# First norm's weight as one row spread by a matmul, convolution blocks split in column halves with rounded products first, small bank copies ahead of the statistics

## The reference

```
h    = rms_norm(x, mix_norm)                      # the first norm
proj = h @ w_in     # u | v | z | xBC | dt | gate_a | gate_b
y_a  = sgu_branch(u, v)        # gelu; layer_norm(v); u * (W_s v + b) in groups of 128
y_b  = mamba2_branch(z, xBC, dt)   # causal conv + silu on xBC, chunked scan, gated norm
x    = x + (sigmoid(gate_a) * (y_a @ w_branch_a) + sigmoid(gate_b) * (y_b @ w_branch_b)) @ w_out
x    = x + moe_ffn(rms_norm(x, ffn_norm))         # 32 experts, top 4, clamped SwiGLU
x    = x + sigmoid(rms_norm(x, ple_norm) @ w_ple_gate) * (p @ w_ple_proj)
out  = rms_norm(x, final_norm)
```

## Time and profile before

| | |
|---|---|
| median of 3 runs | 1320.26 us |
| profiled execution, its own time | 1319.52 us |
| its span, first to last instruction | 1317.5 us |
| PE busy / PEld busy | 1236.3 us (94%) / 654.5 us (50%) |
| DVE / ACT / POOL busy | 351.2 (27%) / 236.2 (18%) / 188.2 us (14%) |
| read from HBM | 456.29 MB, 347 GB/s over the span |
| chain that ended last | DMA 48%, PE 47%, DVE 2%, the rest 3% |

### The profile page before, as it was taken

The page is one execution under the profiler, slowest core; times in us unless marked ns, Lnnn a source line. Parts: engine busy times, 40 slices in busy tenths (PEclk is TensorE's granted clock), DMA queues, the critical chain, the costliest instruction groups (busy, mean ns, idle before and its releaser), DMA issues.

```text
span 1317.5 us, 15399 instructions
## 1 busy us (share of the span) xinstructions
PE 1236.3 (94%) x6309; PEld 654.5 (50%) x6309; DVE 351.2 (27%) x672; ACT 236.2 (18%) x283; POOL 188.2 (14%) x55
## 2 busy tenths in 40 slices
PE   5998999987999999999999999999999999999976
PEld 5986888865444444443334433333334433333342
DVE  3528650434112112121111221211112211211132
ACT  4654444422001000010000000100000000100011
POOL 5855548830000000000000000000000000000000
PEclk9988999997799999999999999999999999999989
DMA  8543357755599999999999999999999999999910
GB/s 266 191 135 122 127 184 298 282 188 226 219 415 428 429 429 428 428 428 428 429 430 429 427 428 428 429 429 429 428 428 428 429 429 429 428 428 428 428 70 32
DMA packets 61350, 457.67 MB, mean 347 GB/s; under 512 B 6800, under 2 KB 16368, under 8 KB 36752
## 3 DMA queue, kind: packets, MB, share of 16 engines
q1 hardware_dynamic: 61328, 457.36, 84.5%
HBM read 456.29 MB, written 1.05 MB: 347 GB/s over the span
## 4 chain that ended last, share of the span: by engine, by line
DMA 48%; PE 47%; DVE 2%; issue 1%; ACT 1%; SPq 0%; POOL 0%; DVEq 0%; ACTq 0%
DMA wring<-in_w_dram 46%; PE bank L825 15%; PE bank L586 6%; PE bank L587 6%; PE bank L588 6%; PE bank L855 4%; PE bank L802 3%; PE bank L926 2%; PE bank L811 1%; PE bank L573 1%; PE bank L690 1%; PE bank L874 1%; PE bank L712 1%; DMA z<-in_mix_norm_dram 0%; PE bank L831 0%
## 5 line engine op out<-in xcount | busy, mean ns | idle before, releaser
L825 PE MATMUL bank<-wring,hT 128*64 128x512 f32 x2048 | 456.8, 599 | 29.0 <-DMA wring<-in_w_dram 29.0
L825 PEld LDWEIGHTS bank<-wring,hT 128*64 128x64 f32 x2048 | 140.4, 137 | 324.0 <-issue 256.5
L855 PE MATMUL bank<-wring,xbcT 128*64 128x512 f32 x1024 | 226.8, 595 | 0.0
L547 POOL TENSOR_TENSOR blk_lo<-blk,blk_hi 128x2048 fp32r<-128x2048 f32 (+1 forms) x41 | 185.9, 4545 | 88.5 <-ACT blk_hi L944 75.8
L855 PEld LDWEIGHTS bank<-wring,xbcT 128*64 128x64 f32 x1024 | 70.7, 137 | 152.1 <-issue 152.1
L1485 DVE TENSOR_SCALAR xbcT<-bank 128x512 f32<-128x512 f32 x32 | 22.1, 692 | 463.2 <-PE bank L831 463.2
L802 PEld LDWEIGHTS bank<-xbcT,ga 128*128 128x128 f32 x1056 | 126.2, 196 | 5.1 <-issue 2.3
L802 PE MATMUL bank<-xbcT,ga 128*128 128x64 f32 x1056 | 124.9, 278 | 1.8 <-issue 1.8
L1104 ACT ACTIVATE xbcT<-xbcT 128x512 f32<-128x512 f32 x32 | 20.2, 630 | 501.4 <-DVE xbcT L1485 501.4
L944 ACT ACTIVATE blk_hi<-blk 128x2048 fp32r<-128x2048 f32 x39 | 74.6, 1915 | 112.8 <-DMA blk<-in_w_in_dram 71.7
L1499 DVE COPY xbcT<-bank 128x256 f32<-128x256 f32 x32 | 13.6, 425 | 270.7 <-PE bank L860 270.7
(11 more groups left out here) (229 smaller groups left out, 944.5 us busy)
## 6 DMA issues: line engine op xcount, KB each, us to landing
wring<-in_w_dram SPq DMA_DIRECT2D x192, 2048.0 KB, 21.7
blk<-in_w_in_dram SPq DMA_DIRECT2D x28, 1024.0 KB, 5.2
blk<-in_w_branch_a_dram SPq DMA_DIRECT2D x4, 1024.0 KB, 5.1
blk<-in_w_branch_b_dram SPq DMA_DIRECT2D x4, 1024.0 KB, 6.1
blk<-in_w_out_dram SPq DMA_DIRECT2D x4, 1024.0 KB, 5.1
blk<-in_w_ple_gate_dram SPq DMA_DIRECT2D x4, 1024.0 KB, 9.1
x<-in_x_dram SPq DMA_DIRECT2D x4, 512.0 KB, 5.1
v<-in_w_ple_proj_dram SPq DMA_DIRECT2D x1, 1024.0 KB, 9.0
```

The lines of the kernel that those rows point to most:

```text
L547: nc.gpsimd.tensor_tensor(dst, raw, hi.bitcast(FP32), ALU.subtract).then_inc(done, 1)
L825: last = mm(bank[dh * SLOTS:(dh + 1) * SLOTS, :], xgT[:, k, :], wring[:, 2 * c + kk, off + dh * W:off + (dh + 1) * W], start=(k == 0), sto ...
L855: last = mm(YB[dh * SLOTS:(dh + 1) * SLOTS, :], actT[:, kk * P + c * SLOTS:kk * P + (c + 1) * SLOTS], wring[:, at, (kk % 2) * D + dh * W:( ...
```

## The change

Three things are changed, and nothing else in the kernel.

1. The weight of the first norm is loaded as one row into one partition, as the first DMA, instead of as 128 copies behind x. PE spreads it over the partitions by two matmuls with a row of ones into banks 6 and 7; DVE applies the norm from there, in halves of 512 columns, and PE starts to transpose a half as soon as it is there. Both sums of squares are made by ACT.
2. The eight xBC blocks are rounded and subtracted in two column halves each. PE makes the eight products of rounded with rounded for a column half first, then those with `blk_lo`, then those with a_lo, and the first column half of block 0 is rounded ahead of a_hi.
3. DVE's small bank copies are placed between the statistics of v's first half and those of its second.

```diff
-            for t in range(TT):
-                load(x[:, t, :], x_in[0, t * P:(t + 1) * P, :], x_loaded[t])
-            load(mix_gain, vec(mix_norm), mix_loaded)
+            load(mix_row, mix_norm, mix_loaded)
+            for t in range(TT):
+                load(x[:, t, :], x_in[0, t * P:(t + 1) * P, :], x_loaded[t])
...
+            pe.wait_ge(mix_loaded, 16)
+            for h in range(HALVES):
+                last = mm(banks[6 + h][:, :], ones[0:1, :], mix_row[:, h * W:(h + 1) * W], start=True, stop=True)
+            last.then_inc(gain_spread, 1)
             for t in range(TT):
-                pe.wait_ge(xn_done, t + 1)
                 for h in range(2):
+                    pe.wait_ge(xn_done, 2 * t + h + 1)
                     transposes(("xT", t, h), ...)
-            wait_taken(pe, *all_of("xT"))
+            pe.wait_ge(act_high, 4)
...
-                        pe.wait_ge(xbc_low, i + 2 if i else c + 1)
+                        pe.wait_ge(blk_high, rounded(i, c))
                         for k in range(KT):
+                            mm(to, col(high(i), k), a_hi[:, k, :], start=(k == 0), stop=False)
+                        pe.wait_ge(xbc_low, 2 * i + c + 1)
+                        for k in range(KT):
+                            mm(to, col(raw_lo, k), a_hi[:, k, :], start=False, stop=False)
+                        if i == 0 and c == 0:
+                            wait_taken(pe, *all_of("xT"))
+                        for k in range(KT):
+                            last = mm(to, col(high(i), k), a_lo[:, k, :], start=False, stop=(k == KT - 1))
...
-            act.wait_ge(x_loaded[0], 16)
-            fn(u[:, 0, :], x[:, 0, :], ACT.Square, accum_out=ssq[:, 0:1]).then_inc(ssq_done, 1)
+            for t in range(TT):
+                act.wait_ge(x_loaded[t], 16)
+                fn(u[:, t, :], x[:, t, :], ACT.Square, accum_out=ssq[:, t:t + 1]).then_inc(ssq_done, 1)
...
-            act.wait_ge(xn_done, TT)
+            split(0, [0])
+            act.wait_ge(xn_done, 2 * TT)
             high_parts("xT", a_hi)
-            split(0)
+            split(0, [1])
...
-            stt(u[:, 1, :], x[:, 1, :], 1.0, x[:, 1, :], ALU.mult, ALU.mult, accum_out=ssq[:, 1:2])...
-            for t in range(TT):
-                stt(v[:, t, :], x[:, t, :], rstd[:, t:t + 1], mix_gain, ALU.mult, ALU.mult)...
+            dve.wait_ge(gain_spread, 1)
+            for t in range(TT):
+                for h in range(HALVES):
+                    cols = slice(h * W, (h + 1) * W)
+                    stt(v[:, t, cols], x[:, t, cols], rstd[:, t:t + 1], banks[6 + h][:, :], ALU.mult,
+                        ALU.mult).then_inc(xn_done, 1)
...
             for b in range(HALVES):
+                if b:
+                    take_small()    # the memset, five copies and the acs subtraction, as before
                 for t in range(TT):
                     wait_taken(dve, ("v", b, t))
                     last = nc.vector.bn_stats(vstat[:, t, b, :], v[:, t, b * W:(b + 1) * W])
```

More of the change, by code:

```diff
@@ L219, in build @@
         ssm_gain = xc[:, 3072:4096].rearrange("p (g n) -> p g n", g=GROUPS)
-        mix_gain = z[:, 0, :]
+        mix_row = z[0:1, 0, :]
         fnorm = z[:, 0, :]
@@ L270, in build @@
         mix_loaded = sem("mix_loaded")
+        gain_spread = sem("gain_spread")
         ssm_loaded = sem("ssm_loaded")
@@ L390, in weights_used, with rounded, column_half @@
                 wait_filled(eng, (kind, b, 1))
+        def rounded(i, c=1):
+            return 2 * i + c + 1 if i < XBC_HALVES else XBC_HALVES + i + 1
+        def column_half(ap, c):
+            return per_k(ap)[:, :, c * P:(c + 1) * P]
         def high(i):
@@ L547, in subtract @@
                 nc.gpsimd.tensor_tensor(dst, raw, hi.bitcast(FP32), ALU.subtract).then_inc(done, 1)
[L550 to L556, removed]
+            for i in range(XBC_HALVES):
+                for c in range(2):
+                    pool.wait_ge(blk_high, rounded(i, c))
+                    subtract(column_half(blk_lo[:, i % NB, :], c), column_half(blk[:, i % NB, :], c),
+                             column_half(high(i), c), xbc_low)
+                if i == XBC_HALVES - 3:
                     pool.wait_ge(wdt_high, 1)
                     subtract(wdt_lo[:], wdt.rearrange("p k h -> p (k h)"), wdt_hi[:], wdt_low)
-                pool.wait_ge(blk_high, i + 2)
-                subtract(blk_lo[:, i % NB, :], blk[:, i % NB, :], high(i), xbc_low if i < XBC_HALVES else nat_low)
+            for i in range(XBC_HALVES, SPLIT):
+                pool.wait_ge(blk_high, rounded(i))
+                subtract(blk_lo[:, i % NB, :], blk[:, i % NB, :], high(i), nat_low)
         @block.tensor
@@ L624, in _ @@
                     for c in range(2):
-                        pe.wait_ge(xbc_low, i + 2 if i else c + 1)
+                        col = lambda ap, k: ap[:, k * TOKENS + c * P:k * TOKENS + (c + 1) * P]
+                        to = bank_of(name)[:, c * TOKENS:(c + 1) * TOKENS]
+                        raw_lo = blk_lo[:, i % NB, :]
+                        pe.wait_ge(blk_high, rounded(i, c))
                         for k in range(KT):
[L628 to L631, removed]
+                            mm(to, col(high(i), k), a_hi[:, k, :], start=(k == 0), stop=False)
[6 more added lines that the diff above has]
+                            last = mm(to, col(high(i), k), a_lo[:, k, :], start=False, stop=(k == KT - 1))
                     last.then_inc(full(name), 1)
@@ L769, in _ @@
             for t in range(TT):
-                pe.wait_ge(xn_done, TT + t + 1)
+                pe.wait_ge(xn_done, 2 * TT + t + 1)
                 for h in range(2):
@@ L911, in _ @@
             for t in range(TT):
-                pe.wait_ge(xn_done, 2 * TT + t + 1)
+                pe.wait_ge(xn_done, 3 * TT + t + 1)
                 for h in range(2):
@@ L934, in _, with split @@
             fn = nc.scalar.activation
-            def split(i):
+            def split(i, parts=range(2)):
                 act.wait_ge(blk_loaded[i % NB], 16 * (i // NB + 1))
[L939 to L942, removed]
+                if i < XBC_HALVES:
+                    for c in parts:
+                        fn(column_half(high(i), c), column_half(blk[:, i % NB, :], c), ACT.Copy).then_inc(blk_high, 1)
                 else:
@@ L1179, in low_parts @@
                            ALU.subtract).then_inc(empty(name), 1)
-            dve.wait_ge(x_loaded[1], 16)
-            stt(u[:, 1, :], x[:, 1, :], 1.0, x[:, 1, :], ALU.mult, ALU.mult, accum_out=ssq[:, 1:2]).then_inc(ssq_done, 1)
             norm(0, None)
-            dve.wait_ge(mix_loaded, 16)
+            dve.wait_ge(gain_spread, 1)
             for t in range(TT):
-                stt(v[:, t, :], x[:, t, :], rstd[:, t:t + 1], mix_gain, ALU.mult, ALU.mult).then_inc(xn_done, 1)
+                for h in range(HALVES):
+                    cols = slice(h * W, (h + 1) * W)
+                    stt(v[:, t, cols], x[:, t, cols], rstd[:, t:t + 1], banks[6 + h][:, :], ALU.mult,
+                        ALU.mult).then_inc(xn_done, 1)
             low_parts("xT", a_hi, a_lo, 0)
@@ L1239, in _, with take_small @@
             cp(dtx[:, 5], dtx[:, 0]).then_inc(empty(("dt",)), 1)
+            def take_small():
+                link(nc.vector.memset(sgu_wT[CHUNK:P, :, 0:CHUNK], 0.0))
+                for h in range(2):
+                    name = ("sguw", h)
+                    wait_filled(dve, name)
+                    cp(sgu_wT[0:CHUNK, 4 * h:4 * h + 4, :], seg4(bank_of(name)[0:CHUNK, :]))
+                    cp(sgu_wT[CHUNK:P, 4 * h:4 * h + 4, CHUNK:P], seg4(bank_of(name)[CHUNK:P, :])[:, :, CHUNK:P]).then_inc(empty(name), 1)
+                name = ("acs",)
+                wait_filled(dve, name)
+                both = bank_of(name)[:, 0:TT * 2 * HEADS].rearrange("p (c a h) -> p c a h", c=TT, a=2)
+                link(cp(acs[:, :, 0, :], both[:, :, 0, :]))
+                tt(acs[:, :, 1, :], both[:, :, 1, :], acs[:, :, 0, :], ALU.subtract).then_inc(acs_done, 1)
+                dve.wait_ge(acs_done, 1)
+                cp(dtx[:, 5], dtx[:, 0]).then_inc(empty(name), 1)
             for b in range(HALVES):
+                if b:
+                    take_small()
                 for t in range(TT):
@@ L1251, in _ @@
             nc.vector.reciprocal(ssq[:], ssq[:]).then_inc(v_var, 1)
[L1253 to L1266, removed]
             def heads(ap):
```

## The result

| | before | changed |
|---|---|---|
| median of 12 runs each | 1320.31 us | 1323.63 us (1322.31 to 1324.82) |
| profiled execution, its own time | 1319.52 us | 1323.78 us |
| its span | 1317.5 us | 1322.0 us |
| POOL / DVE busy | 188.2 / 351.2 us | 189.6 / 360.9 us |

The medians differ by 3.3 us; by the ratio it is 3.6 us. The forecast was 1324.0.

A forecast was written before the change was run, and what follows sets the result against it. The end is set by the experts' load stream, which earlier shifts move one to one; -5.5 + 7.5 + 2.2 = +4.2 on 1319.52 gives 1323.7, said as 1324 for the median; forecast 1321.5 to 1327 (0.62), range 1314 to 1328.

The forecast's parts named there:

- Start: Kernel's start: first xBC product at 13.0, 4.6 us earlier, plus 0.9 saved at half speed; -5.5 us, between -1 and -7.
- The gap ahead of u goes: Ahead of u: banks 2 and 3 free before PE wants them; the 5.6 us wait and 2.5 us at low clock go.
- `v_done` late: Ahead of mix: DVE's eleven wide operations alternate with five POOL subtractions, delaying mix by 7.5 us, between +5.7 and +8.5.
- a sign of being wrong: Ahead of mix: two DVE operations in a row between POOL's beside blocks 16 to 19 would speak against the forecast.
- Cold stretch: At mix: after standing for 15.6 us, PE runs at half rate for a while, costing +2.2 us (0 to 3.4).
- The gap simply closes: Rival ahead of mix: DVE is through at 117.2, mix starts 8.1 us earlier; with the start -13.6, 1306.7 us; chance 0.10.
- Fewer turns: Rival ahead of mix: `v_done` waits for only three subtractions (1316 us) or four (1320 us); chance 0.10 each.
- The start doesn't deliver: Rival at the start: block 0 is late and PE gains 2 at most; 1328 us; chance 0.08.

The follow-up runs named there:

- e1: The changed kernel with the small bank copies back behind the statistics, so the new start alone: 1314.52 us, 0.9961 of before.
- e7: The kernel before with only the xBC blocks in column halves, rounded products first, block 0's first half rounded ahead of a_hi: 1315.8 us, 0.9971.
- e2: The kernel before with only the small bank copies moved between the statistics of v's halves: 1329.46 us, 1.0068 of before.
- e5: The changed kernel without POOL's subtractions for blocks 15 to 19; ACT writes a rounded copy instead, leaving out their low parts: 1307.64 us, 0.9901.
- e3: The changed kernel with the scan's five wide DVE operations moved from ahead of the layer norm to behind the decays, ahead of z's work: 1306.99 us, 0.9902.
- e8: The changed kernel with the scan's five wide DVE operations directly behind the layer norm's six, ahead of cb's copies: 1320.32 us, 1.0002 of before.
- e4: The changed kernel with the small copy L1277 reading the PSUM bank instead of its copy in SBUF: 1321.15 us, 1.0012 of before.
- e6: The kernel before with only the norm's weight as a row spread by matmuls, norm in halves, both square sums on ACT: 1319.24 us, 0.9996.

## Why the prediction was right

- **Start, -5.5.** Right. The first product is at 13.02 (predicted 13.0). The last transposes ahead of u end 6.5 us earlier in the profile (100.25 then, 93.75 now). The 1.9 beyond the product's 4.6 is the clock: the first eight products took 1.21 and the next eight 0.96, where at the low clock the first eight take 2.08 (e1). So PE had the full clock from its first xBC product on, where the earlier trace rows have it from 21.9 on. I had put this stretch at 2.1 and taken 0.9 of it; the rates of the earlier trace rows themselves give 1.9 (20 products at 0.215 rather than 0.119). But e1, of the same start, shows the low clock for longer, and its ratio says -5.1: over its six runs the estimate of 5.5 was good. Block 0 came later than I had read from the earlier trace rows: ACT began to round it at 9.18 (I had it there at 8), and in e7, behind the copies, it landed at 11.24 (I had 9.8). This cost nothing, since the rounding was still over at 10.24, ahead of ACT's first copy into a_hi at 10.60.
- **The gap ahead of u goes.** Right: banks 2 and 3 were free at 92.67, ahead of PE, and the low clock behind it went too.
- **`v_done` late, +7.5.** The mechanism was right, turn by turn, with five subtractions, and the small copy held as taken. The size was too large by about 1: +6.55 in e2, and in the changed kernel mix is 0.25 earlier than in the earlier trace rows with PE at u 6.5 earlier, so +6.25. The term that was mis-sized is the price of a turn, which I had at POOL's whole 4.5. In the changed kernel 33.6 us pass from L1300's start (98.13) to `v_done` (131.73), in e2 33.5 (104.98 to 138.52). The same eleven operations took 12.2 with POOL idle (e5, 100.11 to 112.30). That leaves 21.4 for five turns in either, 4.3 each, where I had 22.5. Part of it is that a held operation ends sooner behind POOL's end than it takes alone (L1303: 1.08 against 1.23 in e5); the rest is open. The order of the last turn was also not as I had listed it: the first L1313 asked at 122.67, block 19's subtraction at 122.69, so L1310 and L1313 ran in a row between two of POOL's, which I had named as a sign of being wrong. It does not matter for `v_done`, since DVE's operations and POOL's subtractions add up in either order: in e2 the subtraction asked first, and a turn costs the same 4.3. That this subtraction ended at 128.25, where the prediction's 134.8 less 6.5 is 128.3, is therefore in part chance: one operation more than listed stood ahead of it.
- **Cold stretch, +2.2.** Right: mix took 5.63 rather than 3.57, +2.1 (e2: +1.8).
- **Sum.** By the ratios the terms stand at -5.1 (e1) and +9.0 (e2) where I had -5.5 and +9.7, and the change at +3.6 where I had +4.2. Both terms were somewhat too large, and as they have opposite signs part of that cancelled. That the profiled execution also ended 4.3 us later, nearly the +4.2, is in part chance: its own terms (-6.5, +6.25, +2.1) give +1.8 at z. The other 2.7 of its span came behind, where the change touches nothing. The router's 32 products at 310 took 0.7 more, at a granted clock of 0.73 rather than 0.86, and the last stage took 2.0 more, at 0.93 rather than 1.00 (last section).
- **Rivals.** "The gap simply closes" was the right price for a kernel without the turns (e5 1307.64, e3 1306.99, against 1306.7), and wrong for this one. "Fewer turns" fell with the five subtractions that POOL began ahead of `v_done`. "The start doesn't deliver" fell with the product at 13.02.

## To carry to other kernels

A wait that is removed ahead of a stage lets that stage's own feeding (loads, rounding, POOL's subtractions) start earlier, on top of the work that the next wait depends on; so count who runs beside whom in the new schedule, not only who is late. Where DVE and POOL share work, the price of a stretch of wide DVE operations on SBUF is their sum plus nearly a whole POOL operation for each that is asked for meanwhile (here 4.3 of its 4.5 to 4.6 us), in whatever order the two come. Put first in DVE's list what PE waits for, put beside POOL what reads PSUM, and keep the operations with SBUF operands alone for when POOL has nothing (e3: 0.9902 of before rather than 1.0027, from the order of five instructions; e8, where they stand ahead of the next thing that PE wants, gives 1.0002).

## What the runs showed of the hardware

- **The turns go by request.** Where DVE and POOL both had a wide operation waiting, each got one in turn, although POOL's takes 4.5 to 4.6 us and DVE's 0.8 to 1.2. The earlier request went first: the first L1313, 0.02 us ahead of block 19's subtraction, took 1.23, and the subtraction 5.56; in e2 the subtraction was 0.10 ahead and took 4.50. The Trainium skill says of the shared port (SBUF — State Buffer, "Who interferes with whom") that whoever issues first holds it for the whole instruction; this case's traces agree, with 9.98 for two L1310 beside POOL and 1.53 in e5 without it.
- **Tiny operations pay the same.** A 128x32 copy took 3.16 beside POOL, 0.18 with POOL idle (L1266 in the trace of before) and 0.19 from the bank; a 128x2 TENSOR_SCALAR 1.19 (e4) where the changed kernel's took 0.17. The statistics were not held: the two that began beside POOL in the trace of before took 1.29, and the two L1284 of the changed kernel, with POOL idle, 1.27. Nor were operations that read PSUM (in e3 16 of L1323 in 4.23, beside POOL).
- **The same code ran at different granted clocks.** The last stage's 64 products, the same code, took 27.75 us in the trace of before and in e1, and 29.72 in the changed kernel. Windows of that stage (columns as in the earlier trace rows), before:

```profile
1279.30:1307.10 27.80, 27.73 (x64) 12.08 (x64) 4.16 (x6) 1.81 (x4) 0.00 (x0) 1.00 0.00 0
```

and the changed kernel:

```profile
1281.90:1311.60 29.70, 29.66 (x64) 12.83 (x64) 4.16 (x6) 1.79 (x3) 0.00 (x0) 0.93 0.00 0
```

At a granted clock of 1.00 and 0.93 the stage differs by 2.0 us. At the start too, one and the same code made its first eight products in 1.21 us in the changed kernel and in 2.08 in e1. So two single executions can differ by 2 us for this reason alone, which is as much as e4 changed; only many runs of both kernels tell such a change apart. The runs of e6 fit this: the five with a granted clock of 0.976 or more over the whole execution took 1316.96 to 1318.67 us, the seven with less 1319.11 to 1320.36. The runs of the kernel before beside them do not part so cleanly.
- **Open.** That the times of e6 and e7 differ from their chains by under 1 us is within this scatter and was not followed up. Why a turn costs 4.3 us and not the whole subtraction is known only in part. That the last stage's low clock comes more often in one kernel than in another was not tested: one profile of each is too few.
